# A two-block transformer layer on one core: the order of the first attention's value and projection tiles, and four small moves elsewhere

## The reference, cut to what matters

```python
# first block
z, xbc, dt_raw, q, k, v, f_raw = split(h @ w_in)          # h = x * (1 + sc1) + sh1
y = ssd_chunked(xs, dt, A, Bm, Cm) + d_skip[:, None] * xs # 4 chunks of 128 tokens, 16 heads
y_ssm = rms_norm(y * silu(z), ssm_norm_w)
y_att = rms_norm(forgetting_attention(q, k, v, log_f), attn_norm_w)   # 16 heads
x = layer_norm(ALPHA * x + (1 + g1) * (concat([y_ssm, y_att]) @ w_out))
x = layer_norm(ALPHA * x + (1 + g2) * (square(relu(h2 @ w_ff_in)) @ w_ff_out))
# second block
p = rms_norm_2(x) @ w_in_2        # q, k, v of 8 heads; gates and input of a short conv; u for pooling
m = window_mean(u, w) - u         # windows 2, 4, 8, 16, then m @ pool_w
x = x + concat([band_attention, gated_conv, pool]) @ w_out_2
x = x + square(relu(rms_norm_2(x) @ w_mlp1)) @ w_mlp2
```

## Time and profile before

| | us |
|---|---|
| median of 3 runs | 1438.65 (1436.66 to 1438.85) |
| the profiled execution | 1433.96 |
| its span, first to last instruction | 1432.2 |
| PE busy in the span | 1370.6 |
| POOL, DVE, ACT busy | 688.3, 698.0, 547.4 |

### The profile page before, as it was taken

The page is one execution under the profiler, slowest core; times in us unless marked ns, Lnnn a source line. Parts: engine busy times, 40 slices in busy tenths (PEclk is TensorE's granted clock), DMA queues, the critical chain, the costliest instruction groups (busy, mean ns, idle before and its releaser), DMA issues.

```text
span 1432.2 us, 17281 instructions
## 1 busy us (share of the span) xinstructions
PE 1370.6 (96%) x6567; PEld 1124.0 (78%) x6567; DVE 698.0 (49%) x1005; ACT 547.4 (38%) x793; POOL 688.3 (48%) x544
## 2 busy tenths in 40 slices
PE   2999999999999999999999998999999999999999
PEld 2887787778777878888888886886788888888887
DVE  6676978788843672141324456357623213132231
ACT  0635454476662262141332316324525223132231
POOL 0453855332346655445445544753644445445442
PEclk9999999999999999999999999999999999999999
DMA  9353445755323432322232232342122332232232
GB/s 331 116 136 93 98 129 173 207 142 150 104 59 130 146 92 88 109 96 88 88 117 88 88 110 72 105 120 77 45 93 89 105 101 88 92 102 99 88 98 78
DMA packets 132249, 158.58 MB, mean 111 GB/s; under 512 B 9469, under 2 KB 93713, under 8 KB 131937
## 3 DMA queue, kind: packets, MB, share of 16 engines
q1 hardware_dynamic: 123760, 146.95, 32.6%
q10 hardware_dynamic: 6240, 5.40, 1.7%
q0 software_dynamic: 2192, 5.49, 1.2%
HBM read 153.47 MB, written 2.26 MB: 109 GB/s over the span
## 4 chain that ended last, share of the span: by engine, by line
PE 81%; DVE 9%; POOL 3%; issue 2%; ACT 2%; DMA 1%; SPq 0%; ACTq 0%; DVEq 0%; POOLq 0%
PE bank L1702 25%; PE bank L1703 24%; PE bank L1704 24%; DVE tmp L1268 3%; POOL w_lo L546 3%; PE bank L1839 1%; DMA arena<-in_w_ada_dram 1%; DVE rinv L1175 1%; PE bank L1970 1%; PE bank L2208 1%; PE bank L1824 1%; ACT w_hi L740 1%; PE bank L1849 1%; PE bank L2026 1%; PE bank L1852 1%
## 5 line engine op out<-in xcount | busy, mean ns | idle before, releaser
L546 POOL TENSOR_TENSOR w_lo<-raw,w_hi 128x512 fp32r<-128x512 f32 x428 | 585.2, 1399 | 605.9 <-ACT w_hi L740 604.7
L1702 PE MATMUL bank<-w_hi,a_hi 128*128 128x512 f32 x928 | 365.3, 394 | 13.3 <-POOL w_lo L546 6.5
L1703 PE MATMUL bank<-w_lo,a_hi 128*128 128x512 f32 x928 | 362.6, 391 | 0.0
L1704 PE MATMUL bank<-w_hi,a_lo 128*128 128x512 f32 x928 | 362.6, 391 | 0.0
L740 ACT ACTIVATE w_hi<-raw 128x2048 fp32r<-128x2048 f32 x107 | 204.7, 1913 | 356.8 <-PE bank L1704 353.6
L1702 PE MATMUL bank<-a_hi,w_hi 128*128 128x512 f32 x800 | 315.7, 395 | 3.4 <-DVE a_lo L1161 2.5
L1703 PE MATMUL bank<-a_lo,w_hi 128*128 128x512 f32 x800 | 312.2, 390 | 0.0
L1704 PE MATMUL bank<-a_hi,w_lo 128*128 128x512 f32 x800 | 312.0, 390 | 0.0
L1702 PEld LDWEIGHTS bank<-w_hi,a_hi 128*128 128x128 f32 x928 | 175.1, 189 | 51.7 <-DVE a_lo L1161 6.2
L1704 PEld LDWEIGHTS bank<-w_hi,a_lo 128*128 128x128 f32 x928 | 175.0, 189 | 36.9
L1703 PEld LDWEIGHTS bank<-w_lo,a_hi 128*128 128x128 f32 x928 | 175.1, 189 | 35.7
(11 more groups left out here) (248 smaller groups left out, 1258.6 us busy)
## 6 DMA issues: line engine op xcount, KB each, us to landing
raw<-in_w_mlp_dram SPq DMA_DIRECT2D x32, 1024.0 KB, 5.3
raw<-in_w_in_dram SPq DMA_DIRECT2D x24, 1024.0 KB, 5.2
arena<-in_w_ada_dram SPq DMA_DIRECT2D x18, 1024.0 KB, 6.5
raw<-in_w_ff_in_dram SPq DMA_DIRECT2D x16, 1024.0 KB, 5.4
raw<-in_w_ff_out_dram SPq DMA_DIRECT2D x16, 1024.0 KB, 5.1
raw<-in_w_out_dram SPq DMA_DIRECT2D x12, 1024.0 KB, 5.6
raw<-in_w_in_dram SPq DMA_DIRECT2D x16, 512.0 KB, 5.7
arena<-in_w_ada_dram SPq DMA_DIRECT2D x3, 2048.0 KB, 18.1
```

The source lines that it names most:

```text
L546: last = pool.tensor_tensor(w_lo[:, u0 % 2, cols], raw[:, u0 % 2, cols], w_hi[:, u0 % 2, cols].bitcast(F32), ALU.subtract)
L1702: pe.matmul(out_, hi_a, hi_b, start=start, stop=False)
L1703: pe.matmul(out_, hi_a, lo_b, start=False, stop=False)
L1704: return pe.matmul(out_, lo_a, hi_b, start=False, stop=stop)
```

## The change

Seven edits, in the order of time:

1. ACT issues `hi(U_Z + 1)` one silu earlier; POOL signals that unit's first three quarters by `z_lo`, and PE's first tile of `z_half(0, 1)` waits quarter by quarter.
2. The multiplication of `xs` by `dsk` leaves `inputs` and stands behind the next chunk's `decay_in`.
3. V's last two units: first `v_half(2, 0)` and `v_half(3, 0)`, then, in steps 0 and 1, `v_half(2, 1)` and `v_half(3, 1)`; banks 0 to 3 in place of 4, 5, 0, 1. `hi(U_QK1)` and the reads of V move with them.
4. Five late slices ahead of the loop in place of six; step 8 gets one.
5. The last projection tiles: `wo1_half(2, 0)`, `(3, 0)`, `(2, 1)`, `(3, 1)` in place of `(2, 0)`, `(2, 1)`, `(3, 0)`, `(3, 1)`, tiles 6 and 7 in banks 6 and 7, both `g_row` in banks 4 and 5; `hi(U_WO2)` moves up in ACT's order, `hi(U_WO1 + 2)` too.
6. `window_sums(1)` and `pooling(1)` go behind the maxima of heads 0 and 1 of the second attention.
7. `band_low` goes behind `output`.

```diff
-V_BANKS = ((4, 5), (0, 1))
+V_BANKS = ((0, 1), (2, 3))
+WO1_BANK = (0, 1, 0, 1, 0, 1, 6, 7)
-LATE_FIRST = 6
-LATE_STEP = (1, 2, 3, 5, 6, 7, 9, 10, 11, 13)
+LATE_FIRST = 5
+LATE_STEP = (1, 2, 3, 5, 6, 7, 8, 9, 10, 11, 13)
...
                 for part in range(4):
                     cols = slice(512 * part, 512 * part + 512)
+                    if part and parts:
+                        last.then_inc(parts, 1)
...
-                if n % 2 and n < CT - 1:
+                if n % 2:
                     hi(U_XBC + n // 2 + 2)
...
             def read_v(d):
 
-                act.wait_ge(ticks, 2 * U_V + 2 * d + 2)
+                act.wait_ge(ticks, 2 * (U_V + 3) + d - 1)
...
-                if s == 2:
-                    read_v(3)
+                if s == 1:
+                    read_v(2)
...
                 if 1 <= s < 17:
                     probabilities(s - 1, score, prob)
+                if s == 1:
+                    read_v(3)
...
-                    link(dve.tensor_tensor(by_head(xs[:, ch]), by_head(xs[:, ch]), per_head(dsk[:]), ALU.mult))
...
                     if ch < TB - 1:
                         decay_in(ch + 1)
+                    link(dve.tensor_tensor(by_head(yc), by_head(yc), per_head(dsk[:]), ALU.mult))
                     dve.wait_ge(y_mm, ch + 1)
...
-            dve.wait_ge(cp_read, 2)
-            window_sums(1)
             for s in range(10):
...
+                if s >= 2:
+                    output(16 + s - 2)
                 if s in (4, 6, 8):
                     band_low(s // 2 - 2)
-                if s >= 2:
-                    output(16 + s - 2)
...
                 if s == 0:
+                    dve.wait_ge(cp_read, 2)
+                    window_sums(1)
+                elif s == 1:
                     pooling(1)
...
             late_columns(1)
+            pe.wait_ge(evac[0], 4 * N_V[0] + 2)
             v_half(2, 0)
             late_columns(2)
-            v_half(2, 1)
+            pe.wait_ge(evac[0], 4 * (N_V[0] + 1))
+            v_half(3, 0)
             late_columns(3)
...
             for s in range(18):
+                if s == 2:
+                    pe.wait_ge(evac[1], 4 * N_V[1] + 4)
...
             wo1_half(2, 0)
             pe.wait_ge(late_made, 1)
             g_row(16, 4)
+            wo1_half(3, 0)
+            pe.wait_ge(g_made, 2)
+            g_row(40, 4)
             wo1_half(2, 1)
-            pe.wait_ge(pt_made, 48)
-            g_row(40, 6)
-            wo1_half(3, 0)
...
-            pe.wait_ge(g_made, 4)
             pe.wait_ge(o_made, 16)
             pe.wait_ge(y_sq, 8)
+            pe.wait_ge(yacc_read, 6)
+            row_pair(U_WO2, 0, N_WO2[0], 0, T_ATT)
+            pe.wait_ge(g_made, 4)
             pe.wait_ge(yacc_read, 8)
-            row_pair(U_WO2, 0, N_WO2[0], 0, T_ATT)
             row_pair(U_WO2 + 2, 1, N_WO2[1], 0)
```

More of the change, by code:

```diff
@@ L997, in wo1_tile @@
                 t, half = n % 4, n // 4
-                act.activation(yacc[:, t, 512 * half:512 * half + 512], bank[n % 2][:], ACT.Copy,
+                act.activation(yacc[:, t, 512 * half:512 * half + 512], bank[WO1_BANK[n]][:], ACT.Copy,
                                scale=st[:, 4 + t:5 + t]).then_inc(yacc_read, 1)
@@ L1014, in _ @@
                     wo1_tile(1)
-                if s == 1:
-                    hi(U_QK1, late=1)
-                elif s == 14:
+                if s == 14:
                     hi(U_WO1 + 1)
+                elif s == 17:
+                    hi(U_WO1 + 2, late=1)
                 if s >= 2:
@@ L1045, in _ @@
                 att_square(pair)
+            for pair in (6, 7):
+                att_high(pair)
+            g_row(0, 4, 0)
+            for pair in (6, 7):
+                att_square(pair)
+            hi(U_WO2)
+            act.wait_ge(ext_out, 32)
+            g_row(1, 4, 3)
             wo1_tile(4)
             wo1_tile(5)
[L1048 to L1053, removed]
             act.wait_ge(square_mm, 1)
             act.activation(st[:, 0:4], bank[2][:, 0:4], ACT.Copy).then_inc(y_sq, 4)
-            act.wait_ge(ticks, 2 * U_WO1 + 7)
-            hi(U_WO2)
-            act.wait_ge(ticks, 2 * U_WO1 + 8)
             for n in (6, 7):
@@ L1800, in wo1_half @@
                     if b == 0:
[L1801 removed]
+                        if d == 3:
+                            pe.wait_ge(pt_made, 48)
+                        elif d:
                             pe.wait_ge(yacc_read, n - 1)
@@ L1806, in wo1_half @@
                         a, w, kk = slice(P * (n % 4), P * (n % 4) + P), slice(512 * k, 512 * k + 512), 4 * b + k
-                        last = three(bank[n % 2][:], a_hi[1][:, kk, a], a_lo[1][:, kk, a],
+                        last = three(bank[WO1_BANK[n]][:], a_hi[1][:, kk, a], a_lo[1][:, kk, a],
                                      w_hi[:, u % 2, w], w_lo[:, u % 2, w], kk == 0, kk == KT - 1)
@@ L1944, in z_half @@
                     for k in range(4):
+                        if (d, b, n) == (0, 1, 0):
+                            if k < 3:
+                                pe.wait_ge(z_lo, k + 1)
+                            else:
+                                pe.wait_ge(w_lo_made, u + 1)
                         a, w, kk = slice(P * (n % 4), P * (n % 4) + P), slice(512 * k, 512 * k + 512), 4 * b + k
@@ L2054, in _ @@
                 if s < 2:
-                    v_half(3, s)
+                    v_half(2 + s, 1)
                 elif s < 14:
                     if s < 4:
-                        pe.wait_ge(evac[1], 4 * N_V[1] + s + 1)
+                        pe.wait_ge(evac[1], 4 * N_V[1] + s - 1)
                     else:
```

25 lines of the change are left out of this document (11 added, 14 removed).

## The result

| | before | changed |
|---|---|---|
| median of the runs compared | 1437.66 (1434.16 to 1438.85) | 1418.04 (1417.40 to 1420.12) |
| ratio, 95% interval | | 0.9868 (0.9849 to 0.9887) |
| the profiled execution | 1433.96 | 1418.40 |
| its span | 1432.2 | 1416.7 |
| mean granted TensorE clock, profiled execution | 0.994 | 0.996 |

The account below looks back on a forecast made before the run. TensorE, busy 1370.6 of 1432.2 us, was taken as the bound; only its idle and half-clock time could be won. Terms 2.1 + 2.7 + 3.3 + 6.8 = 14.9, taken from the median 1438.65, gave 1423.8; range 1419.5 to 1430.0.

Parts of the forecast that it names:

- the sum: Whole kernel: gains of 2.1, 2.7, 3.3 and 6.8 us in four places, together 14.9.
- The first rival: Half clock comes back elsewhere behind waits that stay; both 1.7 terms lost, gain 11.5, time 1427.2; chance 0.18.
- A: Gate and scan: waits of 1.66 and 1.5 go, 1.1 is paid; gain 2.1 us, bounds 1.0 and 3.2.
- B: Value tiles and first attention: V's wait of 2.30 and a 0.4 wait go; gain 2.7, bounds 2.0 and 3.7.
- D: Second attention: waits of 2.92 and 2.16 and 1.7 of half clock go; gain 6.8, bounds 3.8 and 6.8.
- The 1.66: Second gate unit: TensorE's wait of 1.66 us for its last quarter goes whole.
- the price of the moved multiplication: Third and fourth gate units: POOL's splits lose time to the moved skip multiplication, 1.1 us, between 0 and 2.19.
- the 1.5 for the scan: Scan: two waits of TensorE for decay products, 1.5 us in all, taken as gone.
- The price of 0 for the late slice of step 8: First attention, step 8: the added late slice costs 0 of a possible 1.53 us, starting before POOL's split.
- C: Last projection tiles: 0.67, 1.85 and 1.7 of half clock go, new wait 0.9; gain 3.3, bounds 1.0 and 4.2.
- The second rival: Second attention: window sums only move the wait from head 0 to head 1; gain 10.3, time 1428.4; chance 0.09.
- The third: First attention's loop: seven of eleven late slices meet POOL's splits, costing 19.9 us, time 1443.7; chance 0.03.

Follow-up runs that it names:

- The new look at the kernel before: The kernel before, profiled once more without an edit; this execution took 1437.93 us at a clock of 0.992.
- the trace of B: Kernel before with only V's tiles, the late slices and the order of ACT's reads changed; measured 1431.69 us, ratio 0.9962.
- the best one: Changed kernel with the fourth gate unit and U_WO2+1 also signalled by quarters, late slice of step 6 moved to step 12; 1414.72 us, ratio 0.9839 to the kernel before.

## Why the prediction missed

**The step that failed** is the last one, "The median of the runs is 1438.65, 4.69 above the profiled one; taken from it the sum gives 1423.8." It treated 4.69 us as a constant around the kernel, and counted none of it among what the change can win. It was half clock, by all that the later runs show: more of it in the three timed runs than in the profiled one, behind waits that the change removes. (Their own clocks were not recorded; of their times, 1436.66 to 1438.85, two lie among those of the later runs with low clocks and one beside them.) The new look at the kernel before shows where such stretches fall: around chunk 3's product, V's unit and step 9's output, three waits that the sum counted at their length alone. Two of them are gone from the changed kernel, and the third is 0.82 long. Its profiled execution stands where its runs do (1418.40 against a median of 1418.04). The sum taken from the profiled execution gave 1419.1, 1.1 off. The first rival had half of this: it said that a wait may or may not be followed by half clock, but drew from it only a loss.

In averages, from the table above: of the 5.8 that the forecast was too high, 2.3 are the base itself, since the median of three runs, 1438.65, lay that far above the mean of the 52 later runs; 1.8 are waits (13.3 less at full clock, for 11.5 in the sum); and 1.3 are half clock (4.7 less, for 3.4). The low end of the range stood on the same base. That the 14.9 of the sum came near to 15.56 is in part luck: A gave 0.8 less, B 1.9 more, and 0.7 went in places that the sum does not have.

Two bounds have no term behind them: B's upper one of 3.7, which B passed, and D's lower one of 3.8, where its own terms (1.0 and 1.7) give 4.1.

**A** was 1.3 for 2.1 in the sum: 1.84 of waits by the end of the scan, less 0.50 that TensorE loses at 201.63. Of these the traces show 0.34 as idle time; it stands in every kernel with the moved multiplication and in none without it. The 1.66 went whole and the price of the moved multiplication was 0.97 for 1.1: it ran 2.29 beside POOL, and the eight splits took 16.76 for 15.82. Too good was the 1.5 for the scan: chunk 3's product still waits 0.82. Left unsized was that without the move chunk 0's product would be late by 1.10. In the kernel without the move the eight splits took 12.97, 3.8 less, which is more than the multiplication's own 2.29; they began later there and beside other DVE work, so the shares are not told apart. The rule of the Trainium skill that was weighed there (SBUF — State Buffer, Who interferes with whom: one of the two held for a whole instruction) had the direction right, for the price was 0.97 and not 0; that it is the whole multiplication is not shown, as the split's own time went up by more.

**B** was the mis-sized term: 2.7 in the sum, 4.6 between the profiles of before and after, 4.2 at full clock and 5.5 in time alone. Only 0.4 was booked for the small waits of the first steps; four of them, 2.2 in all, are gone from the trace of B. The price of 0 for the late slice of step 8 was right for step 8 and wrong for the loop: what left step 10 came back in step 6.

**C** came as computed: 0.67 and 1.85 gone, 0.78 new for 0.9, the half clock behind it gone, 3.4 by the profiles for 3.3.

**D** came as computed, 7.0 for 6.8. The 2.92 went, but with no slack: TensorE asks 0.24 behind the end of the last exponential. The second rival is refuted, since head 1's scores have no wait. The third, late slices that meet splits, is real at 1.49 in one place and not seven. The four parts make 16.3; 0.5 of it was lost before the gate, where the transposes went over to full rate at 39.9 us for 38.6, and 0.2 in the first feed-forward stretch: 15.6.

## What to carry to other kernels

Before a median is forecast, set each run's mean granted clock beside its time. Where they move together, the runs differ by stretches of half clock, and a change that removes waits removes some of these too: take the sum from the profiled execution with the stretches that its own trace shows (it can be of either kind: 1433.96 or 1437.93 here), and expect the spread to shrink with the waits. A wait of 1 to 3 us should be priced at its length plus a share of 1.7 us (3.4 where the stretch is one of 6.8), whether or not this one profile shows half clock behind it. The share differs from place to place, so several profiles are needed for it. An edit whose waits cancel in the sum (the skip's move) can still be worth some 3 us if it takes away the one that the clock falls behind.

## What the runs showed of the hardware

- The same kernel, with the same waits to within 0.5 us, had half clock behind its waits of 1.85, 2.24 and 2.92 us in one execution, and behind 1.19, 2.30 and 2.16 in another. The span went from 1432.2 to 1436.2 by it.
- How often it came, over the traces of all the kernels here that have the wait: 1.66 us at the second gate unit 0 of 7; 1.18 at chunk 3 1 of 6 (for 6.8 us); 2.30 at V 3 of 6; the stall of 1.5 in the first attention 0 of 11; 1.85 at U_WO2 3 of 5; 2.24 for `a_lo` 13 of 14; 2.92 in the second attention 4 of 5; 2.16 at step 9 1 of 5; 5.98 for `a_lo` 14 of 14. So neither does a wait of this length bring it each time, nor is its length alone what decides: 1.66 never had it and 1.10 had it in the one trace that has that wait.
- Two times of one kernel, 1433.5 and 1439.1, each with about half of 52 runs and few between, with clocks of 0.994 to 0.995 and 0.988 to 0.992. The kernels with fewer waits are narrower: 1417.2 to 1420.3 in nine runs, and 1414.2 to 1415.0 in five of the best one.
- Four DVE instructions with SBUF inputs (0.5 us each) beside the start of a POOL split took 2.01 when clear of it, 2.92 or 3.99 when it met them: steps of about 1 us, with less than 0.1 us between the phases of the two traces that show 2.92 and 3.99.
